# A two-layer decoder step on one core: the samples' top-k sorted in four segments, prompt heads grouped across key heads, sample pairs interleaved

## The chip, the core and the metric

The program runs on one core of a Trainium2 chip. The metric is the device time of one execution in microseconds (us), taken as the median of three runs. A profile is a recording of one such execution. PE is the engine for matrix products, DVE the vector engine, ACT the engine for activation functions, POOL and SP two more that here mostly issue transfers. Each engine works through its own list of instructions in order, and the engines wait for one another by semaphores.

## What is computed

One step of a two-layer decoder for 256 prompt tokens (one sequence) and 32 sample tokens (8 sequences of 4, each with 1024 past keys in pages). Layer 0 is sparse attention and a dense feed-forward block, layer 1 a state space layer and 8 experts. The change lies in the attention of layer 0. An indexer scores every key, the best k are kept (64 for a prompt token, 256 for a sample token), and softmax attention runs over the kept keys, 16 query heads on 4 key heads:

```python
def indexer_topk(qi, wi, ki, q_pos, ksel):
    s = jnp.einsum('bthd,bsd->bths', qi.astype(jnp.float32), ki.astype(jnp.float32))
    score = jnp.einsum('bths,bth->bts', jax.nn.relu(s), wi.astype(jnp.float32)) * INDEX_SCALE
    key_pos = jnp.arange(ki.shape[1])
    score = jnp.where(key_pos[None, None, :] <= q_pos[None, :, None], score, -jnp.inf)
    _, idx = lax.top_k(score, ksel)
    return idx

def sparse_attend(q, kg, vg, idx, q_pos):
    ...
    logits = jnp.einsum('btngd,btsnd->btngs', qg, kg.astype(jnp.float32)) * ATTN_SCALE
    valid = (idx <= q_pos[None, :, None])[:, :, None, None, :]
    p = jax.nn.softmax(jnp.where(valid, logits, -jnp.inf), axis=-1)
    out = jnp.einsum('btngs,btsnd->btngd', p, vg.astype(jnp.float32))
```

The kernel doesn't gather: it adds a large negative number to the logits of the keys that were not chosen.

## The kernel before

All 288 tokens go through the program together, stage by stage: projections and sample scores (to 92 us of the profiled execution), prompt scores (to 124), the top-k and the key norm (to 165), the prompt's attention (to 267), the samples' attention (to 319), output projection, dense block, state space layer, experts.

**Prompt scores.** 16 iterations, 8 for each block of 128 queries. PE makes the products of two index heads (`p_index`, L599), ACT applies the relu (`p_relu`, L1098) into one of four buffers, and DVE adds them, weighted, to the scores (L1565 and L1567). PE has chunks of the query projection between the iterations. ACT's relu of iteration `it` waits until DVE has added iteration `it - 4` (semaphore `pi_acc`). The projections of keys and values (L627) wait for the last relu.

**Top-k.** `topk` (L1550) takes the 8 largest of a row with MAX8 and strikes them out with MATCH_REPLACE, 8 rounds of it for a prompt block of 128 rows and 128 or 256 keys. The samples need 32 rounds over 32 rows of 1056 keys: `ROUNDS_FIRST` = 8 of them stand after the prompt's, and `ROUNDS_EACH` = 3 in each of the 8 prompt groups. What is struck out is what was chosen (`sel`).

**The prompt's attention.** A group (`groups`) is one key head with its four query heads and one block of 128 queries; block 1 has 256 keys, block 0 has 128. For a group PE makes the logits (`p_logits`, L655: for each head the mask by `negid` and then a product over 64 rows), DVE the maxima (`p_max`), ACT the exponentials (`p_exp`), DVE the scaling (`p_norm`), PE the transposes and ACT their copy (`p_turn`), PE the product with the values (`p_values`), DVE the copy out (`p_out`). In PE's list the logits of group i stand before the transposes and values of group i - 1; on DVE the three rounds stand between `p_max(i)` and `p_norm(i)`.

**The samples' attention.** Four pairs of sequences (`bp`), 128 rows (2 sequences x 64) against 1056 keys, with `s_logits` (L697), `s_max`, `s_exp`, `s_values` (L721: transposes, values and the transposes back). PE's order is logits 0, logits 1, values 0, values 1, and the same for 2 and 3. Pairs 0 and 3 share one place in the arena for keys and values, pairs 1 and 2 lie in the ring that holds weights before and after. SP loads the keys page by page (16 transfers a pair), POOL the values. The keys of pair 3 wait for the logits of pair 0 (`sl_mm` at 1), its values for the values of pair 0 (`so_mm` at 1). Then SP loads three units of weights when `so_mm` is 2 and three more when it is 3.

## Time and profile before

| | us |
|---|---|
| median of three runs | 1620.38 (1619.38 to 1622.37) |
| the profiled execution | 1620.28 |
| its span, first to last instruction | 1618.5 |
| prompt's attention, first key transpose to the samples' first logits | 164.9 to 268.6 |
| samples' attention, first logits to the first subtraction after them | 268.6 to 319.2 |

PE is busy for 89% of the span, DVE for 70%, ACT for 52%. The time outside the span is 1.8 us. In the rows below a start is in us from the span's start. The granted clock is that of PE, as a share of its full 2.4 GHz: 1.00 or, at the lower level of 1.2 GHz, 0.50; a stretch with both has a value between. A product of 32-bit numbers shows as two records. In brackets stands how long the engine had been idle before and what ended that.

### The profile page before, as it was taken

The numbers are of one execution on the slowest core, as the hardware profiler recorded it, in microseconds if no ns is written. First come the engines' busy times: TensorE is split into PE (matmuls) and PEld (weight loads), VectorE is DVE, ScalarE is ACT, GpSimd is POOL, SyncE is SP. The second block draws the span as 40 slices with busy tenths as digits, with TensorE's granted clock in tenths as the row PEclk, the third lists the DMA queues.
The fourth block names the chain that finished last, engine by engine and source line by source line (L and its number), as shares of the span: only waits on it lengthen the run. The fifth ranks groups of instructions, "written<-read, shape, count | busy, mean of one in ns | idle before, by whom it ended". The sixth has DMA issues, their size and how long they took to land.

```text
span 1618.5 us, 27656 instructions
## 1 busy us (share of the span) xinstructions
PE 1443.4 (89%) x10549; PEld 1285.7 (79%) x10549; DVE 1138.1 (70%) x1592; ACT 843.3 (52%) x1254; POOL 358.3 (22%) x388
## 2 busy tenths in 40 slices
PE   6996666679999977988499999999999999999995
PEld 4756332378999977888499999999999999999994
DVE  4139885236655446864478888889888888888883
ACT  2221221334344335543277777777777777777772
POOL 3022200208899940100100110303003030020000
PEclk9998557889999997999699999999999999999998
DMA  7432500833556663426159999999999999999980
GB/s 254 178 104 83 143 1 26 312 118 117 183 222 226 227 237 106 157 87 240 42 209 364 347 379 363 374 359 359 379 354 371 361 371 368 350 377 361 372 348 15
DMA packets 67630, 398.25 MB, mean 246 GB/s; under 512 B 8227, under 2 KB 29795, under 8 KB 39587
## 3 DMA queue, kind: packets, MB, share of 16 engines
q1 hardware_dynamic: 56626, 364.89, 59.7%
q0 software_dynamic: 9088, 29.37, 6.0%
q10 hardware_dynamic: 1776, 2.14, 0.4%
q8 instruction: 87, 1.43, 0.3%
q14 instruction: 53, 0.43, 0.1%
HBM read 379.42 MB, written 16.95 MB: 245 GB/s over the span
## 4 chain that ended last, share of the span: by engine, by line
PE 80%; DVE 11%; ACT 4%; issue 3%; DMA 1%; POOL 0%; POOLq 0%; SPq 0%; ACTq 0%; DVEq 0%
PE ps L968 11%; PE ps L969 10%; PE ps L970 10%; PE ps L521 5%; PE ps L991 5%; PE ps L993 5%; PE ps L992 5%; PE ps L523 5%; PE ps L522 5%; PE ps L509 4%; DVE arena L1553 2%; DVE arena L1552 2%; PE ps L501 2%; DVE ring_lo L1437 1%; PE ps L792 1%
## 5 line engine op out<-in xcount | busy, mean ns | idle before, releaser
L969 PE MATMUL ps<-ring_lo,split 128*128 128x256 f32 x1056 | 298.9, 283 | 0.0
L968 PE MATMUL ps<-split 128*128 128x256 f32 x944 | 269.9, 286 | 1.5 <-DVE split L1871 1.5
L970 PE MATMUL ps<-split 128*128 128x256 f32 x944 | 268.1, 284 | 0.0
L1437 DVE TENSOR_TENSOR ring_lo<-ring,chunk_hi 128x1024 fp32r<-128x1024 f32 x100 | 135.2, 1353 | 154.7 <-ACT chunk_hi L1045 154.4
L1819 DVE TENSOR_TENSOR ring_lo<-ring,split 128x2048 fp32r<-128x2048 f32 x88 | 201.7, 2292 | 45.0 <-ACT split L1296 44.5
L1045 ACT CAST chunk_hi<-ring 128x1024 fp32r<-128x1024 f32 x100 | 104.8, 1049 | 217.1 <-PE ps L523 169.8
L969 PEld LDWEIGHTS ps<-ring_lo,split 128*128 128x128 f32 x1056 | 200.1, 189 | 4.7
L968 PEld LDWEIGHTS ps<-split 128*128 128x128 f32 x944 | 179.9, 191 | 5.8 <-issue 1.9
L523 PE MATMUL ps<-xn_lo,chunk_hi 128*128 128x288 f32 x608 | 183.4, 302 | 0.0
L970 PEld LDWEIGHTS ps<-split 128*128 128x128 f32 x944 | 180.0, 191 | 0.0
L1296 ACT CAST split<-ring 128x2048 fp32r<-128x2048 f32 x88 | 169.1, 1922 | 0.0
L521 PE MATMUL ps<-xn_hi,chunk_hi 128*128 128x288 f32 x480 | 148.6, 309 | 19.2 <-DVE xn_lo L1409 12.7
L1891 DVE TENSOR_TENSOR ring_lo<-ring,split 128x1024 fp32r<-128x1024 f32 x132 | 161.0, 1220 | 4.4 <-ACT split L1339 4.4
L991 PE MATMUL ps<-split 128*128 128x512 f32 x352 | 153.5, 436 | 1.1 <-DVE split L1885 1.1
L1328 ACT ACTIVATE arena<-ps 128x128 f32<-128x128 f32 x176 | 48.8, 277 | 194.3 <-PE ps L970 194.3
L522 PE MATMUL ps<-xn_hi,ring_lo 128*128 128x288 f32 x480 | 144.5, 301 | 0.0
L1339 ACT CAST split<-ring 128x1024 fp32r<-128x1024 f32 x132 | 139.5, 1057 | 3.2 <-PE ps L993 3.2
L993 PE MATMUL ps<-split 128*128 128x512 f32 x352 | 138.8, 394 | 0.0
L968 PE MATMUL ps<-chunk_hi,split 128*128 128x256 f32 x464 | 132.4, 285 | 0.0
L970 PE MATMUL ps<-chunk_hi,split 128*128 128x256 f32 x464 | 131.3, 283 | 0.0
L2100 POOL DMA_INDIRECT y<-arena x8 | 12.8, 1601 | 479.4 <-DVE arena L1912 479.4
L1819 DVE TENSOR_TENSOR ring_lo<-ring,chunk_hi 128x2048 fp32r<-128x2048 f32 x44 | 100.8, 2292 | 24.4 <-ACT chunk_hi L1296 24.2
(310 smaller groups left out, 3446.5 us busy)
## 6 DMA issues: line engine op xcount, KB each, us to landing
ring<-wmoe SPq DMA_DIRECT2D x132, 1536.0 KB, 8.8
arena<-wmoe SPq DMA_DIRECT2D x44, 1536.0 KB, 8.6
ring<-wpre SPq DMA_DIRECT2D x41, 1536.0 KB, 7.3
s_b<-arena POOLq DMA_DIRECT2D x8, 640.0 KB, 3.3
arena<-s_b SPq DMA_DIRECT2D x8, 640.0 KB, 3.9
arena<-ck SPq DMA_DIRECT2D x32, 128.0 KB, 3.0
arena<-cv POOLq DMA_DIRECT2D x32, 128.0 KB, 3.1
ring<-ck SPq DMA_DIRECT2D x32, 128.0 KB, 3.5
```

Of the source, the lines that this page charges most:

```text
L521: mm(out, chunk_hi[:, c % 2, w], hi[:, k, :], start=(k == 0), stop=False)
L522: mm(out, lo[:, w], hi[:, k, :], start=False, stop=False)
L523: m = mm(out, chunk_hi[:, c % 2, w], xn_lo_at[:, k, :], start=False, stop=(k == KD - 1))
L968: mm(o, xg_hi[:, e % 2, k, :], hi[:, c], start=(k == 0), stop=False)
L969: mm(o, xg_hi[:, e % 2, k, :], lo[:, c], start=False, stop=False)
L970: m = mm(o, xg_lo[:, e % 2, k, :], hi[:, c], start=False, stop=(k == KD - 1))
L991: mm(o, ht_hi[:, f % 2, :], wd_hi[:, f % 2, c], start=(j == 0), stop=False)
L993: m = mm(o, ht_lo[:, f % 2, :], wd_hi[:, f % 2, c], start=False, stop=(j == NF - 1))
L1296: cp(wg_hi(f), moe_slot(slot)[:, 0:2 * CH]).then_inc(S["chunk_hi"], 1)
L1437: V.tensor_tensor(ring_lo[:, n % RING, w], ring[:, n % RING, w], chunk_hi[:, c % 2, :], ALU.subtract).then_inc(S["chunk_lo"], 1)
L1819: V.tensor_tensor(moe_slot_lo(slot)[:, c], moe_slot(slot)[:, c], wg_hi(f), ALU.subtract).then_inc(S["chunk_lo"], 1)
L1891: V.tensor_tensor(moe_slot_lo(slot)[:, c], moe_slot(slot)[:, c], wd_hi[:, f % 2, :], ALU.subtract).then_inc(S["d_lo"], 1)
```

## The change

**The samples' top-k.** The 1056 scores of a token are cut into four segments of 264, which lie side by side on 128 partitions (the last two with their sign turned). 33 rounds of MAX8 and MATCH_REPLACE sort each segment wholly (`sort_round`); they stand between the instructions of the prompt's scores, one before them and two in each of the 16 iterations. Then two bitonic merges keep the upper 256: `merge_first` makes two lists of 256, eight `sort_stage` calls (two in each of the first four groups) sort them, `merge_last` takes the larger of both and their least element. `ties`, `tie_ranks` and `choose` (one in each of the groups 5, 6 and 7) compare all scores with that element and write `sel`.

**The order on DVE.** The top-k of prompt block 0 stands before the key norm as before; that of block 1 has moved behind the first `p_max`, and the logits of group 0 wait for the first alone.

**Prompt groups** are now two query heads of two key heads and one block of queries, so that products over the partitions 0 to 63 and 64 to 127 follow each other. On PE the logits run one group further ahead, and the values of group i - 1 stand before the transposes of group i.

**Sample pairs.** The logits are made in two pieces (past keys, then new keys), and PE's order is interleaved. The values of pair 3 go to the place of the indexer's and the query's tiles and wait for `sel`, the last logits of the prompt and `qb`. SP's list has not changed.

```diff
+SEG = NKEY // 4
@@
         elif bp == 3:
-            eng.wait_ge(S["so_mm"], 1)
+            eng.wait_ge(S["sel"], 1)
+            eng.wait_ge(S["pl_mm"], 8)
+            eng.wait_ge(S["qb"], 1)
@@ PE, p_logits
+            for gg in range(2):
+                for r in range(2):
+                    o = ps[:, 2 * (i % 2) + r, gg * 256:gg * 256 + nk]
+                    mm(o, negid, selp[:, qk, 0:nk], start=True, stop=False)
+                for r in range(2):
+                    o = ps[:, 2 * (i % 2) + r, gg * 256:gg * 256 + nk]
+                    m = mm(o, q[64 * r:64 * r + 64, 4 * p + 2 * gh + gg, qk * 128:(qk + 1) * 128], kt[64 * r:64 * r + 64, p, 0:nk],
+                           start=False, stop=True)
@@ PE, p_values
             for kb in range(qk + 1):
-                m = mm(ps[64 * r:64 * r + 64, 6 + i % 2, :], vn[:, kb, n * 64:(n + 1) * 64],
-                       v(B_PB + 2048 + (i % 2) * 1024, 2, 512)[:, kb, :], start=(kb == 0), stop=(kb == qk))
+                for r in range(2):
+                    n = 2 * p + r
+                    m = mm(ps[64 * r:64 * r + 64, 6 + i % 2, 0:256], vn[:, kb, n * 64:(n + 1) * 64],
+                           v(B_PB + 2048 + (i % 2) * 1024, 2, 512)[:, kb, r * 256:(r + 1) * 256], start=(kb == 0), stop=(kb == qk))
@@ PE, order of the groups
+        p_logits(0)
         for i in range(9):
-            if i < 8:
-                p_logits(i)
+            if i < 7:
+                p_logits(i + 1)
             if i:
                 p_values(i - 1)
+            if i < 8:
+                p_turn(i)
@@ PE, order of the sample pairs
-        for bp in (0, 2):
+        for bp in range(2):
             s_logits(bp)
-            s_logits(bp + 1)
-            s_values(bp)
-            s_values(bp + 1)
+            s_logits_new(bp)
+        s_turn(0)
+        s_logits(2)
+        s_values(0)
+        s_back(0)
+        s_turn(1)
+        s_logits(3)
+        s_logits_new(2)
+        s_values(1)
+        s_back(1)
...
@@ DVE
+        def sort_round(n):
+            best = seg_l[:, 8 * n:8 * n + 8]
+            link(V.max(best, seg_w))
+            link(V.match_replace(seg_w, best, seg_w, GONE))
...
+        def sort_stage(k):
+            h = 128 >> k
+            src, to = (merge[(k + 1) % 2][0:64].rearrange("p (a b c) -> p a b c", b=2, c=h),
+                       merge[k % 2][0:64].rearrange("p (a b c) -> p a b c", b=2, c=h))
+            V.tensor_tensor(to[:, :, 0], src[:, :, 0], src[:, :, 1], ALU.max)
+            link(V.tensor_tensor(to[:, :, 1], src[:, :, 0], src[:, :, 1], ALU.min))
...
+        def choose():
+            link(V.scalar_tensor_tensor(out=tied[0:NS], in0=ranks[0:NS], scalar=float(TOPK_S), in1=tied[0:NS],
+                                        op0=ALU.is_gt, op1=ALU.mult))
+            V.scalar_tensor_tensor(out=sel[0:NS, :], in0=sc[0:NS, :], scalar=least, in1=tied[0:NS],
+                                   op0=ALU.is_lt, op1=ALU.max).then_inc(S["sel"], 1)
...
                 m.then_inc(S["pi_acc"], 1)
+                sort_round(2 * it + 1)
                 dve.wait_ge(S["pi_acc"], it + 1)
+                sort_round(2 * it + 2)
...
-        topk(sc[0:NS, :], st[0:NS, 112:120], ROUNDS_FIRST)
+        prompt_topk(0)
...
-        for i in range(10):
+        p_max(0)
+        prompt_topk(1)
+        merge_first()
+        for i in range(9):
             if i < 8:
-                p_max(i)
-                topk(sc[0:NS, :], st[0:NS, 112:120], ROUNDS_EACH)
                 p_norm(i)
-            if 2 <= i:
-                p_out(i - 2)
+            if i < 7:
+                p_max(i + 1)
+            if i:
+                p_out(i - 1)
+            if i < 4:
+                sort_stage(2 * i)
+                sort_stage(2 * i + 1)
...
```

The order of the instructions shows three places. The first is DVE at the beginning of the prompt's scores (all tiles lie in the arena, so they read alike; behind the tile stands its shape). Before, the first iterations stand one behind the other:

```order
L1548 MEMSET arena 128x2 [waits dve]
L1565 TENSOR_SCALAR arena<-arena 128x128 [waits pi_relu]
L1567 SCALAR_TENSOR_TENSOR arena<-arena 128x128 [waits dve]
L1567 SCALAR_TENSOR_TENSOR arena<-arena 128x128 [waits pi_relu,pi_acc]
L1567 SCALAR_TENSOR_TENSOR arena<-arena 128x128 [waits dve]
```

Now the copies of the segments, a round, and two rounds in the iteration:

```order
L1599 MEMSET arena 128x2 [waits dve]
L1603 COPY arena<-arena 32x264 x2
L1605 TENSOR_SCALAR arena<-arena 32x264 x2
L1616 MAX arena<-arena 128x8 [waits dve]
L1617 MATCH_REPLACE arena<-arena 128x264 [waits dve]
L1673 TENSOR_SCALAR arena<-arena 128x128 [waits pi_relu,dve]
L1675 SCALAR_TENSOR_TENSOR arena<-arena 128x128 [waits dve]
L1616 MAX arena<-arena 128x8
L1617 MATCH_REPLACE arena<-arena 128x264 [waits dve]
L1616 MAX arena<-arena 128x8 [waits pi_acc,dve]
L1617 MATCH_REPLACE arena<-arena 128x264 [waits dve]
```

Each iteration has gained four instructions on DVE, all of them ahead of the next wait for `pi_relu`, and 4 copies and a round stand ahead of the first.

The second is PE in a prompt group with 128 keys, the last head of the group before included. Before, mask (L666) and product (L667) alternate head by head; transposes (L679) and values (L686) of the group before follow, and then the next logits:

```order
L666 MATMUL ps<-arena 128x256
L667 MATMUL ps<-arena 128x256
L679 MATMUL ps<-arena 128x128 [waits pt_c,pl_n]
L679 MATMUL ps<-arena 128x128 x3
L686 MATMUL ps<-arena 64x512 [waits po,pt_c]
L666 MATMUL ps<-arena 128x128 [waits pl_e]
L667 MATMUL ps<-arena 128x128
```

Now, from the transposes of a group on:

```order
L689 MATMUL ps<-arena 128x128 [waits pt_c,pl_n]
L689 MATMUL ps<-arena 128x128 x3
L675 MATMUL ps<-arena 128x128 [waits pl_e]
L675 MATMUL ps<-arena 128x128
L678 MATMUL ps<-arena 128x128 x2
L675 MATMUL ps<-arena 128x128 x2
L678 MATMUL ps<-arena 128x128 x2
L701 MATMUL ps<-arena 64x256 [waits po,pt_c]
L701 MATMUL ps<-arena 64x256
```

The masks come in twos and the products over 64 rows in twos, and the values of the group before (two products of 256 columns in place of one of 512) stand behind the logits.

The third is PE at the logits of sample pair 3 (`k_in3` counts its keys). Before, with the end of pair 1 ahead of them and all values of pairs 0 and 1 done:

```order
L744 MATMUL ps<-arena 64x256 x2
L748 MATMUL ps<-arena 128x128 [waits so_c]
L748 MATMUL ps<-arena 128x128
L710 MATMUL ps<-arena 128x512 [waits k_in1,so]
L710 MATMUL ps<-arena 128x512
L710 MATMUL ps<-arena 128x32
L717 MATMUL ps<-ring,arena 32x512 x8
L717 MATMUL ps<-arena 32x32 x4
L710 MATMUL ps<-arena 128x512 [waits k_in3,so]
```

Now:

```order
L759 MATMUL ps<-arena 32x128
L718 MATMUL ps<-arena 128x512 [waits k_in3,sl_e]
L724 MATMUL ps<-arena 32x512 x4
L718 MATMUL ps<-arena 128x512
L724 MATMUL ps<-arena 32x512 x4
L718 MATMUL ps<-arena 128x32 [waits so]
L724 MATMUL ps<-arena 32x32 x4
L772 MATMUL ps<-ring,arena 64x256 [waits v_in1,st_c]
L772 MATMUL ps<-ring,arena 64x256 x15
```

The new keys' logits of pair 2 (`so`) and the values of pair 1 (`v_in1`) have moved behind the wait for `k_in3`.

## Rows read from the trace of the kernel before

**Rows 1.** The page, part 4: the chain that ended last, by engine.
```profile
PE 80%; DVE 11%; ACT 4%; issue 3%; DMA 1%; POOL 0%; POOLq 0%; SPq 0%; ACTq 0%; DVEq 0%
```

**Rows 2.** Windows: start:end, length, busy by engine, granted clock, DMA share, GB/s.
```profile
171.00:213.00 42.00, 28.53 (x74) 12.96 (x73) 39.72 (x54) 11.45 (x36) 5.26 (x10) 0.58 0.32 90
213.00:267.00 54.00, 35.98 (x84) 15.28 (x84) 43.17 (x59) 12.09 (x37) 0.00 (x0) 0.56 0.00 0
217.00:223.00 6.00, 5.72 (x9) 1.77 (x10) 5.83 (x8) 0.23 (x1) 0.00 (x0) 0.50 0.00 0
...
292.00:319.00 27.00, 19.38 (x145) 10.29 (x145) 4.17 (x15) 6.90 (x14) 4.83 (x9) 0.87 0.98 390
```

**Rows 3.** Timeline of DVE, scores stage: start, busy, line, op, idle before.
```profile
96.91 0.29 DVE L1565 TENSOR_SCALAR arena<-arena 128x128 f32<-128x128 f32 x1 [3.50 <-ACT arena L1104]
...
124.26 0.29 DVE L1552 MAX8 arena<-arena 128x8 f32<-128x128 f32 x1
```

**Rows 4.** Groups of DVE, 60 to 330 us: count, busy, mean ns, idle.
```profile
L1552 DVE MAX8 arena<-arena 32x8 f32<-32x1056 f32 x32 | 39.9, 1247 | 0.8
...
L1567 DVE SCALAR_TENSOR_TENSOR arena<-arena 128x256 f32<-128x256 f32 x15 | 7.3, 485 | 6.6 <-ACT arena L1104 6.1
...
L1567 DVE SCALAR_TENSOR_TENSOR arena<-arena 128x128 f32<-128x128 f32 x15 | 5.3, 352 | 6.7 <-ACT arena L1104 6.2
...
L1552 DVE MAX8 arena<-arena 128x8 f32<-128x256 f32 x8 | 3.4, 427 | 0.2
L1553 DVE MATCH_REPLACE8 arena<-arena 128x256 f32<-128x256 f32 x8 | 3.3, 409 | 0.0
```

**Rows 5.** Timeline of PE: key and value projections, then the wait.
```profile
122.03 21.66 PE L627 MATMUL ps<-ring,arena 128*128 128x128 f32 x192 [0.70 <-ACT arena L1104]
143.84 3.70 PE L636 MATMUL ps<-arena 128*128 128x2 f32 x32
...
164.88 1.79 PE L650 MATMUL ps<-arena 128*128 128x128 f32 x6 [16.91 <-DVE arena L1592]
```

**Rows 6.** Timeline of DVE: the last prompt group (i = 7).
```profile
249.57 1.23 DVE L1613 TENSOR_REDUCE arena<-ps 128x4 f32<-128x1024 f32 x1 [1.09 <-PE ps L667]
...
258.77 0.18 DVE L1622 RECIPROCAL arena<-arena 128x4 f32<-128x4 f32 x1
258.98 1.23 DVE L1624 TENSOR_TENSOR arena<-arena 128x1024 f32<-128x1024 f32 x1
```

**Rows 7.** Timeline of PE: scores in pairs, logits at two clocks, one group's end.
```profile
119.23 1.14 PE L608 MATMUL ps<-arena 64*128 64x256 f32 x8
...
199.14 0.70 PE L667 MATMUL ps<-arena 64*128 64x256 f32 x2
...
224.17 1.22 PE L667 MATMUL ps<-arena 64*128 64x256 f32 x2
...
260.26 1.97 PE L679 MATMUL ps<-arena 128*128 128x128 f32 x8 [4.45 <-DVE arena L1624]
263.33 3.67 PE L686 MATMUL ps<-arena 128*64 128x512 f32 x4 [1.10 <-ACT arena L1159]
```

**Rows 8.** Timeline of ACT in the last prompt group.
```profile
251.02 0.56 ACT L1148 ACTIVATE arena<-ps,arena 128x256 f32<-128x256 f32 x1 [9.03 <-DVE arena L1616]
...
253.20 0.59 ACT L1159 COPY arena<-ps 128x512 f32<-128x512 f32 x1
```

**Rows 9.** Timeline of SP's DMA queue: the last sample pair's keys.
```profile
271.87 20.37 SPq L410 DMA_DIRECT2D arena<-ck  x16
```

**Rows 10.** Timeline of PE in the sample pairs: first logits, last logits, last values.
```profile
268.57 0.60 PE L710 MATMUL ps<-arena 32*128 32x512 bf16 x3 [1.56 <-issue]
...
295.06 0.60 PE L710 MATMUL ps<-arena 32*128 32x512 bf16 x3 [1.17 <-DMA arena<-ck]
...
311.62 5.87 PE L744 MATMUL ps<-arena 128*64 128x256 f32 x36 [1.84 <-DMA arena<-cv]
```

**Rows 11.** Timeline of DVE after the sample pairs.
```profile
319.17 2.36 DVE L1437 TENSOR_TENSOR ring_lo<-ring,chunk_hi 128x1024 fp32r<-128x1024 f32 x2
```

More of the change, by code:

```diff
@@ L51 @@
 PI_IN_Q = (4, 3, 3, 3, 3)
-ROUNDS_FIRST, ROUNDS_EACH = 8, 3
+SEG = NKEY // 4
 KIDX_BY_POOL = 4
@@ L677, in p_values @@
             for kb in range(qk + 1):
-                for g in range(G):
-                    m = nc.tensor.transpose(ps[:, 4 + kb, g * 128:(g + 1) * 128],
-                                            v(B_PB + (i % 2) * 1024, G, 256)[:, g, kb * 128:(kb + 1) * 128], ident)
+                for h in range(4):
+                    m = nc.tensor.transpose(ps[:, 4 + kb, h * 128:(h + 1) * 128],
+                                            v(B_PB + (i % 2) * 1024, G, 256)[:, h, kb * 128:(kb + 1) * 128], ident)
             m.then_inc(S["pt_mm"], 1)
+        def p_values(i):
+            p, gh, qk = groups[i]
             pe.wait_ge(S["pt_c"], i + 1)
@@ L1136, in _ @@
             act.dma_start(dr["kiout"][t0:t0 + nt, :], kin[0:nt, i, 0:64]).then_inc(S["act"], 16)
-        groups = [(n, qk) for n in range(4) for qk in range(2)]
+        groups = [(p, gh, qk) for p in range(2) for gh in range(2) for qk in range(2)]
         def p_exp(i):
-            n, qk = groups[i]
+            p, gh, qk = groups[i]
             nk = 128 * (qk + 1)
@@ L1548, in _ @@
         V.memset(st[:, 0:2], 0.0).then_inc(S["sc"], 1)
+        for k in range(4):
+            o = slice(32 * k, 32 * k + 32)
+            if k < 2:
+                m = V.tensor_copy(seg_w[o], sc[0:NS, k * SEG:(k + 1) * SEG])
+            else:
+                m = V.tensor_scalar(seg_w[o], sc[0:NS, k * SEG:(k + 1) * SEG], -1.0, None, ALU.mult)
+        link(m)
         def topk(work, mx, rounds, parts=P):
@@ L1604, in _ @@
         dve.wait_ge(S["rq"], 1)
-        groups = [(n, qk) for n in range(4) for qk in range(2)]
+        groups = [(p, gh, qk) for p in range(2) for gh in range(2) for qk in range(2)]
         def p_max(i):
-            nk = 128 * (groups[i][1] + 1)
+            p, gh, qk = groups[i]
+            nk = 128 * (qk + 1)
             stt = st[:, 16 * (i % 2):16 * (i % 2) + 16]
@@ L1666, in s_done @@
             m.then_inc(S["so"], 1)
-        for bp in (0, 2):
-            s_max(bp)
-            s_max(bp + 1)
-            s_sum(bp)
-            s_sum(bp + 1)
-            s_done(bp)
-            s_done(bp + 1)
+        s_max(0)
+        s_max(1)
+        s_sum(0)
+        s_done(0)
+        s_sum(1)
+        s_max(2)
+        s_done(1)
+        s_sum(2)
+        s_max(3)
+        s_done(2)
+        s_sum(3)
+        s_done(3)
         chunk_low(0)
```

176 lines of the change are left out of this document (110 added, 66 removed).

## The prediction

> **What bounds the kernel now.** The chain that ended last is PE for 80% and DVE for 11% [rows 1]; where DVE's share lies is the question. I read the windows first, then DVE's and PE's timelines of the attention, then SP's queue. From 171 to 267 us DVE is busy for 82.9 of 96 us, PE at a granted clock of 0.58 and 0.56, and the DMA engines do next to nothing in the second of the two windows [rows 2]. What DVE does there is seen in the groups: 32 rounds of MAX8 over 1056 keys take 39.9 us, and their replacements stand beside them with as much [rows 4]; in the last prompt group 7.97 us lie between the end of the maxima (249.57 + 1.23) and the reciprocal, all of it the samples' three rounds but for a small product of about 0.17 [rows 6]. So a round costs 2.60. ACT had been idle for 9.03 us before that group's exponentials [rows 8], PE for 4.45 before its transposes [rows 7]. DVE bounds this stage. In the stage before, PE sat idle for 16.91 us until DVE had the keys normed [rows 5]. Behind 268.6 us it is another matter: PE is busy for 19.38 of 27 us and the DMA engines for 0.98 of the time [rows 2], and PE waits for the keys and the values of the last pair [rows 10]. From 319.17 [rows 11] on nothing is edited, so what the attention gains should reach the end.
>
> **Step 1: the sort joins the prompt's scores.** DVE's part of these runs from 96.91 to 124.26 [rows 3], 27.35 us, of which 6.6 + 6.7 = 13.3 are waits for ACT [rows 4]; its own work is 14.05. A round on 264 columns and 128 partitions: MAX8 and replacement take 0.427 + 0.409 on 256 columns [rows 4], 8 more columns add 0.02, and what a round costs besides is 2.60 less two of about 1.24, some 0.13: 1.0 us. Four copies and the first round fit into the 3.50 us that DVE idled before 96.91 [rows 3]. The other 32 rounds fill the waits, and DVE ends at 96.91 + 14.05 + 32 = 143.0, 18.7 later than before. ACT runs four buffers ahead of DVE, so the last relu comes when four iterations are left: an iteration is 2 x 0.485 [rows 4] and two rounds, 3.0 us, so at 143.0 - 12.4 + 0.6 = 131. Then come the key and value projections, 21.66, and the sums, 3.70 + 0.5 [rows 5]: 156.9; root, reciprocal and two products, an estimate of 2.9, give 159.8. Before, DVE stood between (the block 1 rounds and eight of the samples', 29 us, now gone from there). PE now waits between its chunks and may begin the projections at the lower clock; I add 1.7 as an allowance and take 161.6 for the first key transpose, against 164.88 [rows 5]: **3.3 gained**. If PE stays at 1.00 it is 6, if it falls more often, nothing.
>
> **Step 2: from the first key transpose to the samples' first logits**, 164.88 to 268.57 [rows 5, 10], 103.7 us before.
> The opening now: transposes 1.8, copies 0.9, logits 1.9, maxima 0.95, the block 1 top-k that has moved here (8 rounds of 0.98 and a compare, 8.3), first merge 1.4 (four operations like those of 256 columns), scaling 0.9, wait and maxima of group 1, 2.1: 18.2, with sorting hidden nowhere.
> Then three periods of two groups. DVE and ACT as a ring: exponentials of 256 keys 2.18 (251.02 to 253.20 [rows 8]), scaling 0.18 + 1.23 [rows 6], maxima of 128 keys 0.85, exponentials 1.8, scaling 0.9, maxima 1.23 + 0.16 [rows 6] (those of 128 keys are estimated from half the columns and the same fixed part), 8.6, with semaphores 9.0. Copies out and sorting stages, some 1.5 a group, lie beside the exponentials. PE's own list for two groups: a pair of products on two row halves is read from the prompt's scores, 8 records, which are 4 products of 256 columns, in 1.14 us [rows 7], where one alone takes 0.70 at the full clock and 1.22 at the lower [rows 7]. With masks at an estimated 0.2 and 0.3 each, logits are 1.4 + 2.0 at the full clock and 2.3 + 3.6 at the lower. Values: two products of 512 columns took 3.67 [rows 7], in pairs on two column halves about 1.9, with one block 1.0; at the full clock 1.1 and 0.6. Transposes: 1.97 [rows 7] and 1.1; 1.2 and 0.7. PE's sum is 7.0 at the full clock and 11.9 at the lower. The one is under DVE's ring, the other over it. PE would now be busy nearly all the time, but from 217 to 223 it was busy for 5.72 of 6 us at 0.50 [rows 2]; I take the middle, 9.5, with semaphores 9.8, three times 29.4.
> The tail: exponentials 2.2, scaling 1.45 behind the scan over 1056 keys (0.6 of wait), transposes 1.6, copy 1.0, values 1.5, semaphores: 8.6; the compares for `sel` (two of about 1.25) end within it.
> 18.2 + 29.4 + 8.6 = 56.2: **47.5 gained**. At the full clock throughout it would be 51.4 (52.3 gained), at the lower 64 (39.7 gained).
>
> **Step 3: the sample pairs.** SP's list is as before: the keys of pair 3 start when the logits of pair 0 are done, SP issues them for 20.37 us [rows 9], and PE went on at 295.06, 26.5 us after the first logits [rows 9, 10]. Nothing in the change shortens this. What it moves is PE's list: behind that wait now stand the new keys of pair 2, the values of pair 1, and with them the maxima, exponentials and values of pair 2. While SP issues, PE has pair 0 and the transposes of pair 1 to do and then idles for some 10 us. After the keys: logits 2.1, new keys 0.4, values 5.0 (5.87 at 311.62 [rows 10], which I take as the slow end), out and back 1.0, transposes 1.35, copies 1.4, values 5.0, out and back 1.0, transposes and copies 2.8, values 5.0, the end 1.1: 26.2 or so, against 319.17 - 295.06 = 24.1 [rows 10, 11]. The values of pair 3 are loaded from `sel` on, long before; the 1.84 of their wait [rows 10] is gone and is in the sum. **2.2 lost**: the interleaving by itself pays nothing here.
>
> **What lies in other queues.** POOL's values of pairs 1 and 2 and SP's keys start with the end of the value projections, now 9 to 11 us later, and have some 60 us until their use. The output projection's first units start when the values of pair 1 are done, now about 19 us before the end of the samples and not 27; three units of 1.5 MB at 390 GB/s [rows 2] are 12 us, so they are in time; I take nothing, with 4 us as the upper bound. POOL's work for the state space layer starts behind the output projection, as before.
>
> **The sum.** 3.3 + 47.5 - 2.2 = 48.6. The profiled execution took 1620.28 (0.1 from the median), so **1571.7**, about 1572. All at the good end: 6 + 52.3 - 0.1 gives 1562; at the bad end 0 + 39.7 - 4.5 gives 1585.
>
> **Rivals.**
> *The full clock in the loop.* Denser work on PE holds it at 2.4 GHz: 3.3 + 52.3 - 0.1, 1565. Against it stands the 0.50 at 5.72 of 6 us [rows 2]; for it, that PE's gaps of 4.45 us [rows 7] go. The Trainium skill's page "TensorE: Matmul & The Clock Gate", section "Loop structure matters more than you think", says that the loop nest decides whether matmuls keep the full clock; by that rule 1565 would be the time, and the trace's window from 217 to 223 does not bear it out.
> *The lower clock throughout.* 3.3 + 39.7 - 4.5: 1582.
> *The interleaving pays.* If the last keys came before PE needs them, the 10 us of idling go: 1562. SP's 20.37 us for 16 issues [rows 9] speak against it.
> *The row halves do not run side by side* in the logits, and the clock is low. PE's list for two groups is then as before, 3.75 + 5.9 for logits (four products and masks each), 5.7 for values, 3.1 for transposes: 18.4, three times 8.6 more, and opening and tail longer by 8: 34 on top, 1606. The pairs of the prompt's scores [rows 7] speak against it.
> *Slower: a drain of PE at each change of shape.* A group has about 6 changes between full, half-row and half-column products, 48 in all, on top of the rival before. From 14.5 / 48 = 0.3 us each the kernel loses; at 0.5 it takes 1606 + 24 = 1630. Before, a product at the full clock took 0.70 with such a change on either side [rows 7], which leaves little room. The page "TensorEngine Tiling (Array Packing)", section "Key Properties", of the Trainium skill says that a change of tiling mode drains the engine, without a price; no run here shows one yet.
>
> **How the numbers follow.** Forecast 0.52, full clock 0.15, lower clock 0.17, interleaving pays 0.05, no side by side 0.08, drain 0.03. The range 1559 to 1591 takes in the first four with the bounds of steps 1 and 3 and leaves out the last two and some error. A measurement of this kernel can tell about 0.2% from no change. Faster 0.96, the same 0.01, slower 0.03.
>
> **What would show it.** MAX8 over 264 columns near 0.44 us and no wait for ACT among them; the projections beginning near 131; two groups in 9 to 10 us, with PE's waits short; 20 us of issues between the first pair's logits and pair 3's, PE idle for about 10 in them; the first subtraction near 270. I would be wrong if a round cost more than 1.1 us, if the projections ran at the lower clock throughout, or if the period of two groups were above 12 us.

## The result, and the profile after

The changed kernel takes 1571.8 us (median of four executions, 1571.15 to 1573.45) where the kernel before took 1619.9 (1617.06 to 1622.37) on the same chip: a ratio of 0.971, 95% interval 0.969 to 0.972. The forecast was 1572, range 1559 to 1591. The execution that was profiled took 1573.45, with a span of 1571.6.

On the page the chain that ended last has hardly moved; this is the line that answers to [rows 1].

```profile
PE 81%; DVE 9%; ACT 4%; issue 2%; DMA 2%; SPq 1%; POOL 0%; ACTq 0%; DVEq 0%; POOLq 0%
```

DVE's share of it fell from 11% to 9%. What changed is seen in the attention. The windows of the changed kernel (us from the start; busy time and records of each engine, then granted clock, DMA share, GB/s) answer to [rows 2]: the prompt's loop, the first part of the samples, the wait for the last keys, what follows it.

```profile
173.00:216.00 43.00, 31.81 (x180) 18.39 (x180) 31.90 (x68) 20.39 (x64) 8.58 (x16) 0.78 0.37 109
216.00:234.00 18.00, 16.76 (x130) 6.50 (x128) 4.08 (x11) 5.18 (x11) 8.04 (x15) 0.93 0.60 172
234.00:244.00 10.00, 0.38 (x1) 0.10 (x1) 0.00 (x0) 0.24 (x2) 0.00 (x0) 0.58 0.39 114
244.00:249.00 5.00, 5.00 (x29) 1.01 (x30) 0.07 (x1) 0.00 (x0) 0.00 (x0) 0.50 0.00 0
```

The loop now runs at a mean granted clock of 0.78, where rows 2 had 0.56 to 0.58. Then come 18 us in which PE is nearly full, 10 us in which hardly anything but the DMA is at work, and 5 us at 0.50, the lower level, 1.2 GHz.

The groups of DVE's instructions from 90 to 216 us (line, operation, shapes, count, then busy time and mean ns of one, and what ended the idle time before them), against [rows 4]:

```profile
L1616 DVE MAX8 arena<-arena 128x8 f32<-128x264 f32 x33 | 14.3, 433 | 0.6
L1617 DVE MATCH_REPLACE8 arena<-arena 128x264 f32<-128x264 f32 x33 | 13.8, 417 | 0.0
```

The 32 rounds over 1056 keys are gone, 2.6 us each. Their replacements in the kernel before, which [rows 4] do not show:

```profile
L1553 DVE MATCH_REPLACE8 arena<-arena 32x1056 f32<-32x1056 f32 x32 | 39.3, 1229 | 0.0
```

33 rounds over 264 columns, on 128 partitions at once, take their place, 0.433 + 0.417 and a load of values, about 1.0 with what lies between. They wait for nothing that matters (0.6 us in all).

PE's timeline at the projections, and from the last key transposes on (start, duration, idle time before and who ended it), against [rows 5]:

```profile
128.19 24.06 PE L634 MATMUL ps<-ring,arena 128*128 128x128 f32 x192 [5.13 <-ACT arena L1149]
152.40 3.70 PE L643 MATMUL ps<-arena 128*128 128x2 f32 x32 [0.15 <-PE ps L634]
...
159.39 1.79 PE L657 MATMUL ps<-arena 128*128 128x128 f32 x6 [2.92 <-DVE arena L1703]
```

DVE's timeline in the opening of the loop:

```profile
153.00 0.42 DVE L1696 TENSOR_TENSOR arena<-arena 128x256 f32<-128x256 f32 x1 [5.48 <-ACT arena L1165]
...
164.37 0.69 DVE L1725 TENSOR_REDUCE arena<-ps 128x4 f32<-128x512 f32 x1 [3.65 <-PE ps L678]
```

DVE still idles 5.48 us ahead of the key norm and 3.65 ahead of the first maxima. Behind these maxima stands the top-k of block 1, which ends at 173.46, and PE waits for it.

PE in the samples' attention, against [rows 10], SP's queue with the last keys, against [rows 9], and the end, against [rows 11]:

```profile
216.23 0.60 PE L718 MATMUL ps<-arena 32*128 32x512 bf16 x1
...
232.39 1.15 PE L759 MATMUL ps<-arena 128*128 128x128 f32 x9
243.62 0.58 PE L718 MATMUL ps<-arena 32*128 32x512 bf16 x1 [10.08 <-DMA arena<-ck]
244.13 1.94 PE L724 MATMUL ps<-arena 128*32 128x512 f32 x8
...
248.79 5.59 PE L772 MATMUL ps<-ring,arena 128*64 128x256 f32 x32
```

```profile
221.10 20.37 SPq L417 DMA_DIRECT2D arena<-ck  x16
```

```profile
270.64 2.36 DVE L1488 TENSOR_TENSOR ring_lo<-ring,chunk_hi 128x1024 fp32r<-128x1024 f32 x2
```

From these marks the time can be laid out in five stretches: until the samples' scores are ready (nothing edited), from there to the first key transpose, from that to the first sample logits, from these to the first subtraction, and the rest (nothing edited).

| us | before | after | gained |
|---|---|---|---|
| until DVE reads the samples' scores | 91.98 | 91.32 | 0.7 |
| to the first key transpose | 72.90 | 68.07 | 4.8 |
| to the samples' first logits | 103.69 | 56.84 | 46.9 |
| to the first subtraction | 50.60 | 54.41 | -3.8 |
| to the end | 1299.3 | 1301.0 | -1.6 |

That is 46.9 of span. The same marks are used for each experiment, since the stretch ahead of the first one varies without an edit (last section).

### The profile page after: what moved, and what is told of

Read it like the earlier page. It is cut to its first block, busy times and chain, and to the rows that moved or that the text cites. A ratio compares the mean times of both kernels' runs of the same rounds, so it can differ in the third digit from the quotient of the medians.

```text
span 1571.6 us, 27756 instructions
## 1 busy us (share of the span) xinstructions
PE 1413.5 (90%) x10573; PEld 1274.6 (81%) x10573; DVE 1096.6 (70%) x1627; ACT 843.1 (54%) x1254; POOL 357.9 (23%) x388
## 4 chain that ended last, share of the span: by engine, by line
PE 81%; DVE 9%; ACT 4%; issue 2%; DMA 2%; SPq 1%; POOL 0%; ACTq 0%; DVEq 0%; POOLq 0%
PE ps L1013 11%; PE ps L1014 11%; PE ps L1015 11%; PE ps L528 5%; PE ps L1036 5%; PE ps L1038 5%; PE ps L1037 5%; PE ps L530 5%; PE ps L529 5%; PE ps L516 3%; PE ps L508 2%; DVE ring_lo L1488 2%; PE ps L634 2%; PE ps L837 1%; PE ps L1023 1%
## 5 line engine op out<-in xcount | busy, mean ns | idle before, releaser
L1946 DVE TENSOR_TENSOR ring_lo<-ring,split 128x2048 fp32r<-128x2048 f32 x88 | 201.6, 2291 | 47.3 <-ACT split L1347 46.8
```

Source lines behind the costliest of these rows:

```text
L1946: V.tensor_tensor(moe_slot_lo(slot)[:, c], moe_slot(slot)[:, c], wg_hi(f), ALU.subtract).then_inc(S["chunk_lo"], 1)
```

## Experiments

The theory on trial: the samples' rounds on DVE bounded the loop, taking them out is most of the gain, the groups of two key heads bring the rest, and the overlapped pairs bring nothing, since the last keys hold PE. Rivals: the overlap pays; the groups alone do it; the clock decides. Medians are compared with 1571.8, the changed kernel's. The experiments ran on three chips, on which the kernel before took 1619.8 to 1621.5 us, so such a difference can be off by some 2 us; the stretches between marks are the better measure.

**What the sort is worth.** The samples' top-k goes back into the loop; the groups and the pairs stay changed.

```diff
-                sort_round(2 * it + 1)
-                sort_round(2 * it + 2)
...
         prompt_topk(0)
+        topk(sc[0:NS, :], st[0:NS, 104:112], 8)
...
-            if i < 4:
-                sort_stage(2 * i)
...
+            if i < 8:
+                topk(sc[0:NS, :], st[0:NS, 104:112], 3)
+        V.tensor_scalar(sel[0:NS, :], sc[0:NS, :], -2.0e38, None, ALU.is_gt).then_inc(S["sel"], 1)
```

> The changed kernel, with the samples' top-k as before: 32 rounds over 1056 keys, 8 behind block 0's top-k of the prompt and 3 in each of the eight groups, instead of the sort and its merges; the groups of two key heads and the overlapped pairs stay. Theory (the rounds in the loop are what the change removes; a round is 2.6 us of DVE): 24 rounds come back into the loop, 62 us, less some 12 of merging and selecting that go, and 3 or 4 us come off at the key norm, so 1612 to 1622 us, about 1617. Rival (a large part of the gain is PE's: the new groups make the loop short whatever DVE does): under 1600 us.

It took 1612.1 us (1610.6 to 1614.0), 40 more: the theory's low end, and far from the rival's 1600. Without the sort, all the rest of the change leaves a ratio of 0.994 to the kernel before on that chip (0.992 to 0.996). DVE's timeline in one group, where nothing has an idle time in brackets (of its three rounds the first is shown):

```profile
204.45 0.18 DVE L1724 RECIPROCAL arena<-arena 128x4 f32<-128x4 f32 x1
204.66 1.23 DVE L1726 TENSOR_TENSOR arena<-arena 128x1024 f32<-128x1024 f32 x1
205.81 0.69 DVE L1715 TENSOR_REDUCE arena<-ps 128x4 f32<-128x512 f32 x1
...
206.94 1.24 DVE L1602 MAX8 arena<-arena 32x8 f32<-32x1056 f32 x1
208.21 0.08 DVE L1603 MATCH_VALUE_LOAD arena<-arena 32x8 f32 x1
208.29 1.23 DVE L1603 MATCH_REPLACE8 arena<-arena 32x1056 f32<-32x1056 f32 x1
...
214.81 0.18 DVE L1724 RECIPROCAL arena<-arena 128x4 f32<-128x4 f32 x1
```

From one group's reciprocal to the next it takes 10.36 us (204.45 to 214.81), all of it DVE's, 7.87 for three rounds. PE, with its shorter list, waits 4.2 to 5.6 us a group for DVE's scaling.

**What the groups are worth.** The prompt's groups go back to four heads of one key head, the sort and the pairs stay.

```diff
-        groups = [(p, gh, qk) for p in range(2) for gh in range(2) for qk in range(2)]
+        groups = [(n, qk) for n in range(4) for qk in range(2)]
...
+            for g in range(G):
+                o = ps[:, 2 * (i % 2) + g // 2, (g % 2) * 256:(g % 2) * 256 + nk]
+                mm(o, negid, selp[:, qk, 0:nk], start=True, stop=False)
+                m = mm(o, q[64 * r:64 * r + 64, 4 * p + g, qk * 128:(qk + 1) * 128], kt[64 * r:64 * r + 64, p, 0:nk],
+                       start=False, stop=True)
```

> The changed kernel, with the prompt's groups as before (four heads of one key head, so one row half at a time in the logits and 512 columns on one column half in the values); the sort, the loop's new order and the sample pairs stay. Theory (with the samples' rounds out of the loop, PE's list would become the bound of the loop if the halves did not run side by side): two groups take 12 to 16 us instead of 9.7, and the kernel takes 1580 to 1596 us, about 1588. Rival (DVE and ACT set the period of the loop, and the new groups gain nothing): 1569 to 1575 us.

1580.8 us (1574.4 to 1584.1), 9 more. From the scores to the first sample logits it took 137.2 us, not 124.9. PE in two groups with 256 keys of this kernel, at the two levels of the clock, and then the pair of the changed kernel at the upper one:

```profile
192.13 1.22 PE L675 MATMUL ps<-arena 64*128 64x256 f32 x2
...
194.75 3.27 PE L697 MATMUL ps<-arena 128*64 128x512 f32 x4
...
202.67 0.27 PE L674 MATMUL ps<-arena 128*128 128x256 bf16 x1
202.88 0.70 PE L675 MATMUL ps<-arena 64*128 64x256 f32 x2
...
206.02 1.93 PE L697 MATMUL ps<-arena 128*64 128x512 f32 x4
```

```profile
194.94 0.39 PE L675 MATMUL ps<-arena 128*128 128x256 bf16 x2
195.26 0.70 PE L678 MATMUL ps<-arena 64*128 64x256 f32 x4
195.89 1.08 PE L701 MATMUL ps<-arena 128*64 128x256 f32 x8
```

One product over 256 keys on one row half takes 0.70, two records; the pair on both halves takes 0.70 too, four records. So the halves do run side by side. That makes the step's sign right. Its size was 12.3 us, and not the 34 of the forecast's rival; 7.2 of it lie in the three periods of two groups, for which the rival had 26. The longer list, nearly without gaps, ran at the upper clock from 198 us on (1.22 falls to 0.70, 3.27 to 1.93); the last section has its windows.

**Only the sort.** The groups and the pairs both undone.

```diff
-        groups = [(p, gh, qk) for p in range(2) for gh in range(2) for qk in range(2)]
+        groups = [(n, qk) for n in range(4) for qk in range(2)]
...
-        s_turn(0)
-        s_logits(2)
-        s_values(0)
...
+        for bp in (0, 2):
+            for b1 in (bp, bp + 1):
+                s_logits(b1)
+                s_logits_new(b1)
```

> The changed kernel with both other parts undone, the prompt's groups (as before, four heads of one key head) and the sample pairs (old order): what is left is the sort, its merges and the loop's new order. Theory (the parts add up: the groups as in the run with the groups undone, the pairs as in the run with the pairs in the old order, which was 6.3 us faster): that run's time less 5 to 7 us, 1574 to 1590 us. Rival (the sort alone brings the whole gain, and more without the overlap): 1562 to 1568 us.

1579.1 us (1575.8 to 1582.2). With the three runs a table of the stretch from the samples' scores to their first logits can be made:

| us | old groups | new groups |
|---|---|---|
| rounds in the loop | 176.6 (before) | 164.3 |
| sort in the scores | 137.2, 137.3 | 124.9 |

(The two runs with old groups stand for one cell.) In the changed kernel the sort is worth 39.4 us, from the right column, and the groups 12.3, from the lower row: in each of these comparisons nothing else in the stretch is edited. The other two differences come out alike, but they aren't the same quantities, because the kernel before has the old order of the loop as well. Of the 12.3 in the upper row, 8.2 lie ahead of the first key transpose (72.9 us from the samples' scores, and 64.7 with the rounds put back), where no group runs: that is block 1's top-k, which has moved into the loop. The 12.3 in the lower row lie wholly behind the first key transpose. And where DVE has no idle time and PE waits 4.2 us or more a group, shorter groups on PE can gain little (only DVE's copy of a group's output, 0.42 us and not 0.68, some 2 us in all). So the table doesn't show that the parts are independent of each other, nor what the order of the loop is worth. The rival "groups alone" falls by the 1612.1. The pairs, in this setting, are worth less than expected: the stretch to the first subtraction is 48.5 here and 51.6 with only the groups undone, and the medians differ by 1.7 where both runs scatter by 6 to 10.

**What the overlap is worth.** The changed kernel, the pairs in the old order (on PE, shown here, and likewise on ACT and DVE).

```diff
-        s_turn(0)
-        s_logits(2)
-        s_values(0)
-        s_back(0)
-        s_turn(1)
-        s_logits(3)
...
+        for bp in (0, 2):
+            for b1 in (bp, bp + 1):
+                s_logits(b1)
+                s_logits_new(b1)
+            for b1 in (bp, bp + 1):
+                s_turn(b1)
+                s_values(b1)
+                s_back(b1)
```

> The changed kernel, with the sample pairs in the old order on PE, ACT and DVE (two pairs' logits, then each pair's transposes, values and transposes back; the new banks and the new place of the last values stay). Theory (the interleaving by itself pays nothing, because the keys of pair 3 are issued for 20.4 us behind pair 0's logits and hold PE): from the first sample logits to the first subtraction it takes 22.3 to 24.1 us behind keys that come 27.4 us after the first logits, so 50 to 51.5 instead of 54.4, and the kernel takes 1568 to 1570 us, 2 to 4 less than the changed kernel's 1572. Rival (the interleaving is part of the gain): 1576 to 1582 us, with this stretch at 58 or more.

1565.5 us (1565.4 to 1565.6), 6.3 less: the overlap costs more than the theory had. The stretch to the first subtraction is 49.1 (213.43 to 262.57). PE's timeline around pair 3's logits:

```profile
239.60 1.06 PE L724 MATMUL ps<-ring,arena 128*32 128x512 f32 x8
...
240.91 0.39 PE L718 MATMUL ps<-arena 32*128 32x512 bf16 x1
241.23 1.06 PE L724 MATMUL ps<-arena 128*32 128x512 f32 x8
```

There is no wait at all: while SP issued the keys, PE did the values of pairs 0 and 1 and pair 2's logits, and came to pair 3's 27.5 us after the first logits (the masks at 240.91, the keys' products at 241.23), when the keys were there. Against before (50.6) 1.5 us are gained. The wait of 1.84 us for the last values [rows 10] is gone, which would account for it; that it is the cause was not tried by itself. So the order itself costs 54.4 - 49.1 = 5.3 in this stretch.

**Two ways to take the wait away.** First PE's order alone:

```diff
         s_turn(1)
-        s_logits(3)
         s_logits_new(2)
         s_values(1)
         s_back(1)
         s_turn(2)
+        s_logits(3)
         s_logits_new(3)
```

> The changed kernel, with the logits of pair 3 moved on PE alone from ahead of pair 2's new keys to behind pair 2's transposes, so that pair 1's values and pair 2's new keys and transposes stand ahead of the wait for the last keys. Theory (PE idles 10.1 us for those keys while this work was ready): the work fills the idle time, pair 3's logits begin as the keys land (27.4 us after the first logits), behind them come the values of pair 2 and all of pair 3: some 17.5 us instead of 27.0, so 1562 us (1560 to 1564). Rival (PE's order is not what counts there; ACT or DVE, or the lower clock after a pause, sets the end): 1569 to 1573 us.

1562.1 us (1561.8 to 1563.4), the theory's time, but not by the theory's sum: the stretch to the first subtraction is 46.8, 7.7 less and not 9.5, and in the profiled execution the samples' scores were ready 3.8 us earlier than in the changed kernel's, ahead of any edit. PE's timeline ahead of pair 3's logits and behind:

```profile
229.62 3.67 PE L772 MATMUL ps<-ring,arena 128*64 128x256 f32 x32 [0.44 <-ACT arena L1234]
...
234.73 1.15 PE L759 MATMUL ps<-arena 128*128 128x128 f32 x9
238.91 0.58 PE L718 MATMUL ps<-arena 32*128 32x512 bf16 x1 [3.04 <-DMA arena<-ck]
239.42 1.93 PE L724 MATMUL ps<-arena 128*32 128x512 f32 x8
```

The values of pair 1 and the transposes of pair 2 have moved into the wait, and 3.04 of its 10.08 us are left. Behind it pair 3's logits still run at the lower clock, and PE's work to the first subtraction takes 19.8 where the theory had 17.5. The rival (PE's order doesn't count) falls. Then the place of the keys:

```diff
     def past_keys(b):
-        if b // 2 in (0, 3):
+        if b // 2 == 0:
             return v(B_KV + (b % 2) * 4096, 2, PAST)
+        if b // 2 == 3:
+            return v((B_QI, B_QIB)[b % 2], 2, PAST)
...
         if b // 2 == 3:
-            return v((B_QI, B_QIB)[b % 2] + j * 256, 256)
+            return v(B_KV + (b % 2) * 4096 + j * 256, 256)
...
-            if b == 6:
-                sp.wait_ge(S["sl_mm"], 1)
-            elif b % 2 == 0:
+            if b % 2 == 0:
                 kv_place_free(sp, b // 2)
...
-                kv_place_free(pool, b // 2)
+                if b == 6:
+                    pool.wait_ge(S["sl_mm"], 1)
+                else:
+                    kv_place_free(pool, b // 2)
```

> The changed kernel, with the places of the last pair's keys and values swapped: the keys go where the sort was, and may start with the selection (about 2 us ahead of the first logits and 7 us earlier than now); the values take the place of pair 0's keys and start when pair 0's logits are done, 40 us before their use. No engine's order of work changes. Theory (the landing of the last keys sets the end of the samples): PE's wait of 10.1 us falls to about 3, and the kernel takes 1565 us (1563 to 1567). Rival (keys and values, now issued the other way round, share the DMA engines, so the keys land no sooner, or the values become the wait): 1570 to 1574 us.

1563.5 us (1562.7 to 1572.6). The profiled execution is the longest of these: behind the samples, where nothing is edited, it took 1308.3 us and the changed kernel's 1301.0; the attention can be read all the same. SP's queue, and PE:

```profile
214.30 20.37 SPq L417 DMA_DIRECT2D arena<-ck  x16
```

```profile
237.69 0.58 PE L718 MATMUL ps<-arena 32*128 32x512 bf16 x1 [4.84 <-DMA arena<-ck]
238.20 1.93 PE L724 MATMUL ps<-arena 128*32 128x512 f32 x8
...
240.60 1.61 PE L724 MATMUL ps<-arena 128*32 128x512 f32 x8
...
242.46 3.67 PE L772 MATMUL ps<-ring,arena 128*64 128x256 f32 x32
```

SP's issues take 20.37 us as ever, but PE goes on 3.0 us behind the end of the last issue (234.67 to 237.69), where in the changed kernel it was 2.2 (241.47 to 243.62): 0.9 us that could be the rival's sharing of the DMA engines with the values, which isn't shown. SP starts 1.25 us ahead of the first logits (215.55), not 4.87 behind them, PE waits 4.84 and not 10.08, and the clock comes back before the logits are done (the second half of their products takes 1.61 where the first took 1.93, the values 3.67 and not 5.59). The stretch is 46.9.

**What the wait costs beside itself.** The wait is left as long as it is, and PE is kept busy in it with eleven products that nobody reads.

```diff
         s_turn(1)
+        pe.wait_ge(S["so"], 1)
+        for _ in range(11):
+            mm(ps[:, 2, :], ident, prob[1][:, 0:512], start=True, stop=True)
         s_logits(3)
```

> The changed kernel, with eleven products added on PE between pair 1's transposes and pair 3's logits, into a PSUM bank that is free then (their result is overwritten): some 9.4 us of work at 2.4 GHz in the 10.1 us for which PE waits for the last keys. They compute nothing that is used. Theory (the wait costs twice: 10 us of idling, and behind it pair 3's logits, 4.8 us, and pair 1's values, 6.2 us, at the lower granted clock): PE stays at 2.4 GHz, the logits take 2.9 and the values 4.3, and the kernel takes 1568 us, 4 less than the changed kernel. Rival (the lower clock behind the wait lies beside other work, or doesn't come from the pause): 1571 to 1574 us.

> The changed kernel itself, unedited, on the chip of the run with the filled wait, as the measure for it: 1571 to 1574 us, with the first key transpose between 154.9 and 159.4 us, where the runs with the same code ahead of it lay, and 54.4 us from the first sample logits to the first subtraction.

1569.9 us (1566.6 to 1571.3) against 1573.3 (1571.6 to 1574.2) for the changed kernel on that chip. The latter's stretch to the first subtraction is again 54.41; its first key transpose came at 160.0, a little behind the expected span. With the filled wait the stretch is 50.1. PE's timeline:

```profile
231.53 9.61 PE L792 MATMUL ps<-arena 128*128 128x512 f32 x22
241.63 0.37 PE L718 MATMUL ps<-arena 32*128 32x512 bf16 x1 [0.49 <-DMA arena<-ck]
241.94 1.06 PE L724 MATMUL ps<-arena 128*32 128x512 f32 x8
...
244.56 3.67 PE L772 MATMUL ps<-ring,arena 128*64 128x256 f32 x32
```

The keys come as late as ever, 27.2 us after the first logits, but pair 3's logits take 2.6 us (241.63 to 244.25) and not 4.8 (243.62 to 248.39), and pair 1's values 3.67 and not 5.59. Work that computes nothing makes the kernel faster by 4.3 us in that stretch. What is left of the cost of the order is 1.0 (50.1 against 49.1 for the old one): of the 5.3, the lower clock behind the wait accounts for 4.3. The theory holds, the rival (the lower clock is hidden) falls. The Trainium skill, "TensorE: Matmul & The Clock Gate", section "Loop structure matters more than you think", names a long wait for a DMA ahead of matmuls as what makes them run at the lower clock; these two rows agree.

**DVE's holes.** Block 1's top-k of the prompt goes into the two idle times of the opening.

```diff
         prompt_topk(0)
+        topk(scp[:, 1, 0:256], st[:, 112:120], 5)
         dve.wait_ge(S["kv_ev"], 3)
...
+        prompt_topk(1, 5)
         p_max(0)
-        prompt_topk(1)
         merge_first()
```

(`prompt_topk(1, 5)` does the three rounds that are left, and the compare.)

> The changed kernel, with block 1's top-k of the prompt taken from behind the first maxima: five of its eight rounds go into the time in which DVE waits for the key projections (5.48 us idle), the other three and the compare into the wait for the first logits (3.65 us idle). Theory (DVE's list is the path of the loop's opening, and the sort in the scores left these two holes): 8.3 us of work go into 9.1 us of idle time, the period of two groups stays at 9.3 to 9.9, and the kernel takes 1564 us (1563 to 1566). Rival (PE at the lower clock is the bound from the first group on, and the top-k lay beside its work): 1569 to 1573 us.

1564.9 us (1561.5 to 1566.1), 6.9 less. From the first key transpose to the samples' first logits it took 50.0 us and not 56.8, and DVE's two idle times have shrunk to 0.90 and 0.17. PE at the lower clock was not the bound of the opening; DVE's list was.

**Together.** Pair 3's logits later, the places swapped and the top-k in the holes: the three diffs above at once, of each a line.

```diff
         s_turn(2)
+        s_logits(3)
...
+            return v((B_QI, B_QIB)[b % 2], 2, PAST)
...
+        topk(scp[:, 1, 0:256], st[:, 112:120], 5)
```

> The changed kernel with three edits at once: pair 3's logits behind pair 2's transposes on PE, the places of the last pair's keys and values swapped, and block 1's top-k of the prompt in DVE's two idle times. Theory (the first two treat the same wait of 10.1 us and so add up only in part; the third is elsewhere and adds up in full): alone they gave 9.7, 8.3 and 6.9 us; together PE no longer waits for the last keys, so some 13 us from the first two and 7 from the third: 1552 us (1549 to 1556). Rival (what follows the samples, the units of the output projection or a lower clock, takes the gain back): 1558 us or more.

1549.0 us (1545.7 to 1552.3): 0.955 of the kernel before, interval 0.953 to 0.957, and 22.8 us less than the changed kernel. PE's timeline around pair 3's logits:

```profile
230.18 1.15 PE L759 MATMUL ps<-arena 128*128 128x128 f32 x9
231.26 0.38 PE L718 MATMUL ps<-arena 32*128 32x512 bf16 x1
231.58 1.07 PE L724 MATMUL ps<-arena 128*32 128x512 f32 x8
...
234.20 3.67 PE L772 MATMUL ps<-ring,arena 128*64 128x256 f32 x32
```

No wait, and these products run at 2.4 GHz. The samples take 39.7 us from the first logits to the first subtraction, 14.7 less than in the changed kernel; the opening gives 6.2 (50.65 and 56.84). So the overlap of the pairs does pay, 9.4 us against the old order (49.1), once the keys are there in time and pair 3's logits stand behind the work that is ready. (The old order with the places swapped was not tried. It had no wait for the keys that the swap could take away; that the swap would bring it nothing is argued from that.)

## Why the prediction came out right, and where it did not

**The bound.** DVE's rounds bounded the loop, as read from [rows 4, 6]: putting them back costs 40 us, and DVE then has no idle time in a group.

**Step 1** was to gain 3.3 and gained 4.8, counted from the samples' scores. DVE's part came as put: the rounds take 1.0, and it ends at 141.46 where the sum had 143.0, 0.7 of it from the earlier start. The projections began at 128.19 where the sum had 131: that term was mis-sized. The last relu begins 13.9 us ahead of the end of DVE's part (127.54 and 141.46), and the sum had let it begin 12.4 ahead: the addition that releases it stands ahead of the two rounds of its own iteration, and the sum had counted these before it. They also took 24.06 and not 21.66, the first 6 us of them at a granted clock of 0.56, for which 1.7 had been allowed; it was 2.4.

**Step 2** was to take 56.2 and took 56.84. Opening 18.2 foreseen, 19.05 measured (159.39 to the end of the second maxima at 178.44); two groups 9.8 foreseen, 9.28, 9.71 and 9.87 measured; tail 8.6 foreseen, 8.93 measured. The clock lay between the levels, as chosen: 0.78 over the loop, 0.82 to 0.83 in the three periods. The two rivals on the clock (1565, 1582) would have had 1.0 or 0.5.

But what set the period was not the term that the sum went by. It had taken PE's list at the middle clock, 9.5 and 0.3 for semaphores, with PE's waits short. PE was busy for 7.0 to 7.9 us of a period and idle for about 2. The other term, the ring of DVE and ACT with 9.0, is what the trace shows: take away the one wait of DVE for PE's logits in each period, 0.28, 0.70 and 0.87 us, and 9.00, 9.01 and 9.00 are left. The second of these waits:

```profile
196.01 1.22 DVE L1725 TENSOR_REDUCE arena<-ps 128x4 f32<-128x1024 f32 x1 [0.70 <-PE ps L678]
```

So 9.8 was hit in part by luck: both terms stood in the prediction, and the one that was not chosen, with up to 0.9 on top, came to nearly the same. The price of the rival with the full clock doesn't follow from the terms either: 18.2 + 3 x 9.0 + 8.6 is 53.8, and it had 51.4.

"No side by side" and "a drain" both fall by the pairs: 0.70 for two halves as for one. A price for the change of shape can now be read. At the upper clock two masks over 256 keys take 0.32 from the first one's start to the pair's (194.94 to 195.26), one alone 0.21 (202.67 to 202.88): the second costs 0.11, so 0.10 is the most that the change from the full shape to half rows can cost. For the change back, with the groups undone, a product on 256 columns takes 0.62 until the next mask starts (202.88 to 203.50) and one on 128 columns 0.41 (198.60 to 199.01); 0.20 do not go with the columns, and the change is within them. Both lie under the 0.3 from which that rival would have made the kernel slower. The Trainium skill, "TensorEngine Tiling (Array Packing)", section "Key Properties", says that a change of tiling mode drains the engine; the rows leave room for 0.1 to 0.2 us of that at each change, and show no stall of its own.

A rival's price was wrong in this step too. "No side by side" was put at 34 us; undoing the groups costs 12.3 in this stretch. PE's list had been costed at the lower clock throughout (18.4 for two groups). It took 14.3 in the first two, at the lower clock but with no values of a group with 256 keys among them yet (3.3 us), and 11.3 and 10.5 in the next, with the upper clock from 198 us on.

**Step 3** was to lose 2.2 and lost 3.8. That the last keys hold PE was right: they came 27.4 us after the first logits (26.5 foreseen; SP was released 4.87 us after them and not 3.30; 1.1 of that is the first half of pair 0's logits, which ran at the lower clock, 2.40 us against 1.31 for the second half), PE idled 10.08, and behind the keys it took 27.0 (26.2 foreseen). That 26.2 came so near is in part luck: the logits took 4.8 where the sum had 2.1, and of the three values, put at 5.0 each, the first took 6.2 and the other two 4.25. "The interleaving by itself pays nothing" was too mild. The old order in the same kernel is 5.3 faster in this stretch. The sum had not asked what the wait does to the work behind it; it brought PE to 1.2 GHz, 4.3 us by the filled wait, in the logits and the values behind it. And the sum had not noticed that in the old order PE comes to pair 3's logits when the keys have just landed, without any wait.

**What lies in other queues** was taken at nothing with 4 us as the bound. The stretch behind the samples was 1.6 longer than before; in the twelve profiled executions shown here, with nothing edited there, it lay between 1299.3 and 1308.3, so no cause can be given to 1.6.

The sum 48.6 met 46.9 with errors of +1.5 (step 1), +0.7 (the start), -0.6 (step 2), -1.6 (step 3) and -1.6 (the rest); the large term, 47.5, was the best of them, and the others partly cancelled.

What stays open: how much the loop's new order (block 1's top-k behind the first maxima, the logits one group further ahead) is worth by itself. It was not undone alone, and the table can't tell it, since in the kernel before it goes together with the old groups and the rounds in the loop.

## What to carry to other kernels

When an engine that is late is relieved, cost the lists of all the others at both clocks, and the ring of waits between them, before deciding which one comes next; here the sort was worth 39.4 us and the groups on PE's halves 12.3, each undone alone in the changed kernel, and what set the period in the end was the ring of DVE and ACT. An overlap written into the order of an in-order engine is worth only as much as its latest input allows: place the instruction that waits for the last transfer behind all work that is ready, and start the transfer where a place comes free first (1571.8 to 1549.0 with DVE's holes filled). And a wait can be dearer than its length: PE's 10.08 us for the last keys cost 4.3 more behind them.

## What the runs showed of the hardware

Ten microseconds in which PE waits cost 4.3 more behind them: the logits of pair 3, 4.8 us long, run at a granted clock of 0.50, and at 1.00 when PE is busy through the wait. Behind the wait of 3.04 us, with pair 3's logits later, they took 4.8 us at 0.50 as well.

A PE that is full does not have the upper clock for that. With the groups undone, these are the windows of the loop's first groups and of those behind (columns as above):

```profile
174.00:198.00 24.00, 23.45 (x55) 10.68 (x55) 11.05 (x27) 7.34 (x25) 7.51 (x14) 0.51 0.60 177
198.00:216.00 18.00, 17.51 (x80) 9.28 (x80) 14.59 (x32) 9.51 (x31) 0.00 (x0) 1.00 0.01 1
```

PE was busy for 23.45 of 24 us at 0.51, the lower level, and then for 17.51 of 18 us at 1.00, with the same kinds of work. In the first the DMA engines moved 177 GB/s, in the second nothing; but from 217 to 223 in [rows 2] PE was busy for 5.72 of 6 us at 0.50 with the DMA engines idle, so that alone isn't the cause, and it stays open.

The start of the kernel varies with nothing edited there. The first 48 records of the query projections, in the changed kernel's profiled execution and in that with pair 3's logits later:

```profile
21.85 14.66 PE L516 MATMUL ps<-arena,ring 128*128 128x288 f32 x48 [3.33 <-DVE arena L1476]
```

```profile
20.77 11.91 PE L516 MATMUL ps<-arena,ring 128*128 128x288 f32 x48 [3.33 <-DVE arena L1476]
```

14.66 us against 11.91, at a mean granted clock of 0.79 (21 to 36 us) against 1.00 (21 to 33); the samples' scores were ready at 91.32 and at 87.50. Over the runs it is 87.5 to 92.2. Times from the start of the span can't be compared to a few us; times from a mark can, and from the samples' scores to their first logits six executions with the same code lay within 124.5 and 125.1.
